# A two-block model on one core: first weights moved ahead of x, their second half behind it

## The chip, the cores and the metric

The kernel runs on one core of one Trainium2 chip. The metric is the device time of one execution in microseconds (us). Engines are named as in the profile: PE is TensorE (matmuls; PEld its weight loads), DVE is VectorE, ACT is ScalarE, POOL is GpSimd, SP is SyncE, which issues nearly all DMAs; SPq is its queue. Line numbers are those of the kernel before.

## The reference

One sequence of 512 tokens, 1024 wide, passes two blocks. Only the start of the first concerns this change:

```python
def rmsnorm(x, g):
    y = xf * rsqrt(mean(xf * xf, -1) + 1e-6)
    return y * g
...
h = rmsnorm(x, norm1_g)
u = h @ w_in
...
```

`w_in` is 1024 by several thousand; its columns feed a short convolution, three kinds of attention or state mixing, and gates. After that come an output product, a gated FFN of width 2816, and a second block with windowed attention and spatial gating. All is float32.

## The kernel before

**Products.** x is kept turned: features on the 128 partitions, tokens along the row, as eight blocks of 128x512. Each float32 product is made of three in a rounded type: with w = whi + wlo and h = hh + hl, a tile is the sum over eight blocks of whi·hh + whi·hl + wlo·hh, so 24 matmuls of 128x512 accumulate in one PSUM bank. ACT makes whi (a rounding copy of raw), POOL makes wlo = raw - whi.

**Units.** Weights come in units of 1024 rows by 256 columns (1 MB) into `raw`, which has two slots. A unit has two column halves of 128 columns, each one tile. Unit n uses slot n % 2; SP loads it when `lo_done` says that POOL is through with the slot's last content (`slot_free`). ACT rounds unit n in `split(n)` (line 1142), POOL makes its rest in `rest` (line 528), one count of `lo_done` for each column half. PE works tile after tile (`gemm_fm`, lines 596, 597 and 604), after `hi_done` and `lo_done`. The row scale of the norm is not put on h: PE multiplies x times g, and the scale (rcol, as R in every lane) is multiplied on each tile afterwards.

**The beginning**, which the change touches. x arrives in four pieces (`load_x(q)`, line 357, 512 KB each, semaphore `x_in{q}`), each with the columns of two blocks. PE turns block m of x (`turn_in(m)`, line 673, four transposes) into the bank TURN[m]: the banks are M[0] to M[3], G[1], G[2], G[3] and M[0] again, so block 7 can be turned only when block 0 has been copied out of M[0]. ACT makes hh of the block (line 1172), DVE makes hl (line 1574); these read the bank. Besides, each turned block is copied to xT, unscaled, for later: blocks 0, 4, 5 and 6 by DVE (line 1577, `xg_kept`), the others by ACT (line 1177, `x_kept`).

Unit 0 is special. The first column half of its weights comes in two parts of four row blocks each (`first_weights(q)`, line 370, 256 KB, `first_raw{q}`), which ACT rounds separately (line 1170, `first_hi`), POOL following (line 546). The second column half (line 361, 512 KB, `raw_in0`) is rounded in one piece (line 1174, `hi_done`). SP issues in the order of its program; it holds x's third piece until the first has landed, the fourth until the second has, and the second column half until `first_raw1`; unit 1's 1 MB follows right behind that.

PE's beginning is written out in `first_tile`: nine idle products on a zeroed tile (line 681), blocks 0 and 1, two idle products, blocks 2 and 3, two idle products, then the products of the first tile (lines 703, 704) in the order of k, with blocks 4 and 5 turned ahead of k = 2, and 6 and 7 ahead of k = 4. The parts of whi are waited for at k = 0 and k = 4. From k = 6 on the products with wlo come in between (line 701), after `lo_done`. Then `gemm_fm(1, ...)` computes the second column half, whose first product is the first of line 596; its bank G[1] held turned block 4.

Of the kernel before, what the change touches and what calls it, by code (L numbers as in the profile page):

```python
# [29 lines left out]
KD = DM // P  # L30
# [45 lines left out]
def build_program(nc, x, par, cst1, cst2a, w_in, w_branch, w_o, w_gu, w_down, w_in2, sg_w, sg_b, ln_g,  # L76
                  ln_b, w_ao, w_so, w_o2, out):
    f32, f32r = mybir.dt.float32, mybir.dt.float32r
    ALU, ACT = mybir.AluOpType, mybir.ActivationFunctionType
# [5 lines left out]
    with ctx:  # L85
# [269 lines left out]
        def _(sp):  # L355
# [13 lines left out]
            def first_weights(q):  # L369
                sp.dma_start(raw[:, 0, 4 * q:4 * q + 4, 0:P], cols(w_in, IN_XA, P, 4 * q, 4)).then_inc(sem(f"first_raw{q}"), 16)  # L370

            load_x(0)
            load_x(1)
            first_weights(0)
            sp.wait_ge(sem("x_in0"), 16)
            load_x(2)
            first_weights(1)
            sp.wait_ge(sem("x_in1"), 16)
            load_x(3)
            sp.wait_ge(sem("first_raw1"), 16)  # L380
            load(0, cols(w_in, IN_XA + P, P), raw[:, 0, :, P:])
            for n, c in enumerate(a_cols):
# [193 lines left out]
        def _(pe):  # L576
            mm = nc.tensor.matmul

            def gemm_fm(T, n, s, xh, xl, kts, col, first, whi_=whi, wlo_=wlo, hooks=None, ready=None):

                bank = bank_of(T) if isinstance(T, int) else G[T[1]]
                Tv = T if isinstance(T, int) else T[0]
                if not isinstance(T, int) or T >= 4:

                    pe.wait_ge(sem("tile_free"), free_before(T) if isinstance(T, int) else Tv - 3)
                else:
                    pe.wait_ge(sem("xg_kept"), T + 1)
                if first:

                    pe.wait_ge(sem("hi_done"), n + 1)  # L590
                for k in range(kts):
                    if ready:

                        pe.wait_ge(sem(ready[0]), ready[1] + k + 1)
                    w = whi_[:, s, k, col:col + P]
                    mm(bank[:, :], w, xh[:, k, :], start=(k == 0), stop=False)  # L596
                    mm(bank[:, :], w, xl[:, k, :], start=False, stop=False)  # L597
                    if hooks and 2 * k + 2 in hooks:
                        hooks[2 * k + 2]()
                if whi_ is whi:  # L600

                    pe.wait_ge(sem("lo_done"), 2 * n + 1 + col // P)
                for k in range(kts):
                    last = mm(bank[:, :], wlo_[:, s, k, col:col + P], xh[:, k, :], start=False, stop=(k == kts - 1))  # L604
                    if hooks and 2 * kts + k + 1 in hooks:
                        hooks[2 * kts + k + 1]()
                last.then_inc(sem("tile_done"), 1)
# [60 lines left out]
            def turn_in(m):  # L668
                pe.wait_ge(sem(f"x_in{m // 2}"), 16)
                if m == KD - 1:  # L670
                    pe.wait_ge(sem("xg_kept"), 1)
                for t in range(TT):
                    last = nc.tensor.transpose(TURN[m][:, t * P:(t + 1) * P], xtm[:, t, m * P:(m + 1) * P], ident)
                last.then_inc(sem("xT_ps"), 1)

            def first_tile():

                bank = G[0]
                def idle_products(count):
                    for i in range(count):  # L680
                        mm(bank[:, 0:P], warm, warm, start=True, stop=True)

                pe.wait_ge(sem("warm"), 1)
                idle_products(9)
                pe.wait_ge(sem("ident_in"), 16)
                for m in range(2):
                    turn_in(m)
                idle_products(2)
                for m in range(2, 4):
                    turn_in(m)  # L690
                idle_products(2)
                for k in range(KD):
                    if k in (2, 4):
                        turn_in(k + 2)
                        turn_in(k + 3)
                    if k in (0, 4):
                        pe.wait_ge(sem("first_hi"), k // 4 + 1)
                    if k == KD - 2:
                        pe.wait_ge(sem("lo_done"), 1)
                    for i in {KD - 2: range(0, 4), KD - 1: range(4, KD - 1)}.get(k, ()):  # L700
                        mm(bank[:, :], wlo[:, 0, i, 0:P], hh[:, i, :], start=False, stop=False)
                    pe.wait_ge(sem("h_lo"), k + 1)
                    mm(bank[:, :], whi[:, 0, k, 0:P], hh[:, k, :], start=(k == 0), stop=False)
                    mm(bank[:, :], whi[:, 0, k, 0:P], hl[:, k, :], start=False, stop=False)
                mm(bank[:, :], wlo[:, 0, KD - 1, 0:P], hh[:, KD - 1, :], start=False, stop=True).then_inc(sem("tile_done"), 1)
# [154 lines left out]
            for n in range(N_A):  # L860
                def after(j, n=n):
                    if n == 1 and j == 0:

                        pe.wait_ge(sem("c1_in"), 16)
                        pe.wait_ge(sem("x_kept"), KD - 4)
                        pe.wait_ge(sem("rcol"), 1)
                        for t in range(TT):
                            last = nc.tensor.transpose(M[0][:, t * P:(t + 1) * P], rcol[:, t:t + 1].broadcast_to((P, P)), ident)
                        last.then_inc(sem("r_ps"), 1)
                    run_mix(stages, 2 * n + j)  # L870
                if N_VV <= n < N_VV + 2:
                    wide_unit(n, n - N_VV, tiles_before(N_VV), lambda t: after(t // 2) if t % 2 else None)
                elif n == 0:
                    first_tile()
                    gemm_fm(1, 0, 0, hh, hl, KD, P, True)
                else:
                    unit_fm(n, after=after)
# [247 lines left out]
        def _(act):  # L1125
# [38 lines left out]
            act.preload_act_table_set(EXP_LN)  # L1164
            act.wait_ge(sem("start_in"), 16)
            for m in range(KD):
                if m in (2, 4):
                    q = m // 2 - 1
                    act.wait_ge(sem(f"first_raw{q}"), 16)
                    fn(whi[:, 0, 4 * q:4 * q + 4, 0:P], raw[:, 0, 4 * q:4 * q + 4, 0:P], ACT.Copy).then_inc(sem("first_hi"), 1)  # L1170
                act.wait_ge(sem("xT_ps"), m + 1)
                fn(hh[:, m, :], TURN[m][:, :], ACT.Copy, scale=pcol("g1", m)).then_inc(sem("h_hi"), 1)
            act.wait_ge(sem("raw_in0"), 16)
# [362 lines left out]
        def _(dve):  # L1536
# [35 lines left out]
            for m in range(KD):  # L1572
                dve.wait_ge(sem("h_hi"), m + 1)
                stt(out=hl[:, m, :], in0=TURN[m][:, :], scalar=pcol("g1", m), in1=as_f32(hh[:, m, :]),
                    op0=ALU.mult, op1=ALU.subtract).then_inc(sem("h_lo"), 1)
                for g in {1: (0,), KD - 1: (4, 5, 6)}.get(m, ()):
                    v.tensor_copy(xT[:, g, :], TURN[g][:, :]).then_inc(sem("xg_kept"), 1)

            ts(half_c, pcol("cw", 0, 20), 0.5, None, ALU.mult)
# [653 lines left out]
```

## Time and profile before

| | us |
|---|---|
| median of three runs | 1326.94 (1326.91 to 1326.95) |
| the profiled execution, its own time | 1327.24 |
| its span, first to last instruction | 1325.2 |
| PE busy | 1317.9 |
| POOL busy | 594.0 |
| DVE busy | 575.6 |
| ACT busy | 510.4 |

The profile was taken in one execution. Its span is from the first to the last instruction; the execution's own time is 2.0 us longer. Engines work side by side, so busy times do not add up to the span. PE is busy 99% of it, so the time of this kernel is PE's row of products and the gaps in it.

### The profile page before, as it was taken

The numbers are of one execution on the slowest core, as the hardware profiler recorded it, in microseconds if no ns is written. First come the engines' busy times: TensorE is split into PE (matmuls) and PEld (weight loads), VectorE is DVE, ScalarE is ACT, GpSimd is POOL, SyncE is SP. The second block draws the span as 40 slices with busy tenths as digits, with TensorE's granted clock in tenths as the row PEclk, the third lists the DMA queues.
The fourth block names the chain that finished last, engine by engine and source line by source line (L and its number), as shares of the span: only waits on it lengthen the run. The fifth ranks groups of instructions, "written<-read, shape, count | busy, mean of one in ns | idle before, by whom it ended". The sixth has DMA issues, their size and how long they took to land.

```text
span 1325.2 us, 16981 instructions
## 1 busy us (share of the span) xinstructions
PE 1317.9 (99%) x6504; PEld 1080.5 (82%) x6504; DVE 575.6 (43%) x952; ACT 510.4 (39%) x731; POOL 594.0 (45%) x448
## 2 busy tenths in 40 slices
PE   9999999999999999999999999999999999999998
PEld 8877877888888888888888888877778888888887
DVE  4674544556544333313321345666555322242233
ACT  6223534566433433222211235354555224343233
POOL 4453333443644364444544555433433453435441
PEclk9999999999999999999999999999999999999999
DMA  6333142313223343333333223322222232423321
GB/s 203 96 113 102 43 148 68 124 41 119 80 94 137 95 113 103 100 97 96 95 96 95 87 72 112 104 69 75 94 68 90 95 95 64 127 65 97 99 90 64
DMA packets 144494, 126.70 MB, mean 96 GB/s; under 512 B 4465, under 2 KB 139761, under 8 KB 144433
## 3 DMA queue, kind: packets, MB, share of 16 engines
q1 hardware_dynamic: 144080, 125.66, 30.9%
q8 instruction: 43, 0.70, 0.2%
q10 hardware_dynamic: 352, 0.19, 0.1%
q14 instruction: 19, 0.15, 0.0%
HBM read 120.46 MB, written 2.10 MB: 92 GB/s over the span
## 4 chain that ended last, share of the span: by engine, by line
PE 99%; DMA 1%; ACT 0%; ACTq 0%; SPq 0%; DVE 0%; issue 0%
PE gemm L596 26%; PE gemm L597 26%; PE gemm L604 26%; PE gemm L657 2%; PE gemm L654 2%; PE gemm L653 2%; PE gemm L620 2%; PE gemm L621 2%; PE gemm L626 2%; PE mix L990 1%; PE mix L978 1%; PE mix L967 1%; DMA xtm<-x 1%; PE mix L1044 1%; PE mix L812 1%; PE mix L837 0%
## 5 line engine op out<-in xcount | busy, mean ns | idle before, releaser
L528 POOL TENSOR_TENSOR wlo<-raw,whi 128x512 fp32r<-128x512 f32 x424 | 568.8, 1372 | 549.3 <-ACT whi L1142 549.3
L596 PE MATMUL gemm<-hh,whi 128*128 128x512 f32 x1128 | 443.9, 394 | 0.0
L597 PE MATMUL gemm<-hl,whi 128*128 128x512 f32 x1128 | 439.4, 390 | 0.0
L604 PE MATMUL gemm<-hh,wlo 128*128 128x512 f32 x1128 | 280.2, 390 | 0.0
L1142 ACT ACTIVATE whi<-raw 128x2048 fp32r<-128x2048 f32 x106 | 202.7, 1912 | 201.3 <-PE gemm L604 167.5
L596 PEld LDWEIGHTS gemm<-hh,whi 128*128 128x128 f32 x1128 | 211.8, 188 | 47.9 <-issue 4.2
L597 PEld LDWEIGHTS gemm<-hl,whi 128*128 128x128 f32 x1128 | 211.9, 188 | 43.1 <-issue 0.2
L604 PEld LDWEIGHTS gemm<-hh,wlo 128*128 128x128 f32 x1128 | 211.3, 188 | 43.6
L524 POOL TENSOR_TENSOR wlo_b<-raw_b,whi_b 128x512 fp32r<-128x512 f32 x16 | 20.6, 1288 | 144.8 <-ACT whi L1142 144.8
L1875 DVE TENSOR_TENSOR fu_t<-gemm,R 128x512 f32<-128x512 f32 x22 | 15.2, 692 | 99.7 <-PE gemm L604 99.7
L596 PE MATMUL gemm<-ah,whi 128*128 128x512 f32 x132 | 51.3, 389 | 0.0
L597 PE MATMUL gemm<-al,whi 128*128 128x512 f32 x132 | 51.3, 389 | 0.0
L1818 DVE TENSOR_TENSOR gt<-gemm,R 128x512 f32<-128x512 f32 x32 | 22.1, 690 | 65.2 <-PE gemm L604 65.0
L1159 ACT ACTIVATE gt<-gt 128x512 f32<-128x512 f32 x32 | 20.1, 628 | 71.6 <-DVE gt L1818 71.6
L1340 ACT ACTIVATE fg_t<-fg_t 128x512 f32<-128x512 f32 x22 | 13.9, 633 | 84.7 <-DVE fg_t L1873 84.7
L1894 DVE TENSOR_TENSOR xT<-xT,gemm 128x512 f32 x16 | 10.9, 688 | 70.1 <-PE gemm L604 56.7
L620 PE MATMUL gemm<-whi,hh 128*128 128x512 f32 x96 | 39.1, 408 | 0.0
L621 PE MATMUL gemm<-whi,hl 128*128 128x512 f32 x96 | 37.6, 391 | 0.0
L1882 DVE TENSOR_TENSOR al<-fu_t,ah 128x512 f32 x22 | 34.7, 1575 | 2.7
L1873 DVE TENSOR_TENSOR fg_t<-gemm,R 128x512 f32<-128x512 f32 x22 | 15.2, 692 | 46.4 <-PE gemm L604 39.8
L604 PE MATMUL gemm<-ah,wlo 128*128 128x512 f32 x132 | 32.9, 389 | 0.0
L1385 ACT ACTIVATE wp<-mix,sml 128x256 f32<-128x256 f32 (+1 forms) x64 | 27.8, 455 | 10.5 <-DVE sml L1973 10.5
(454 smaller groups left out, 1854.9 us busy)
## 6 DMA issues: line engine op xcount, KB each, us to landing
raw<-w_in SPq DMA_DIRECT2D x53, 1024.0 KB, 5.3
raw<-w_gu SPq DMA_DIRECT2D x44, 512.0 KB, 5.0
raw<-w_o SPq DMA_DIRECT2D x8, 1024.0 KB, 5.1
raw<-w_down SPq DMA_DIRECT2D x16, 512.0 KB, 3.9
raw_b<-w_branch SPq DMA_DIRECT2D x16, 256.0 KB, 5.8
raw<-w_ao SPq DMA_DIRECT2D x4, 1024.0 KB, 5.1
raw<-w_so SPq DMA_DIRECT2D x4, 1024.0 KB, 5.1
raw<-w_in SPq DMA_DIRECT2D x7, 512.0 KB, 4.6
```

The lines of the kernel that those rows point to most:

```text
L528: last = nc.gpsimd.tensor_tensor(a(wlo), a(raw), as_f32(a(whi)), ALU.subtract)
L596: mm(bank[:, :], w, xh[:, k, :], start=(k == 0), stop=False)
L597: mm(bank[:, :], w, xl[:, k, :], start=False, stop=False)
L604: last = mm(bank[:, :], wlo_[:, s, k, col:col + P], xh[:, k, :], start=False, stop=(k == kts - 1))
L620: mm(o, hh[:, 4 * half + i, tok], w, start=(half == 0 and i == 0), stop=False)
L621: mm(o, hl[:, 4 * half + i, tok], w, start=False, stop=False)
L626: last = mm(o, hh[:, 4 * half + i, tok], w, start=False, stop=(half == 1 and i == 3))
L653: mm(bank[:, :], w, xh[:, k, :], start=(k == 0), stop=False)
L654: mm(bank[:, :], w, xl[:, k, :], start=False, stop=False)
L1142: fn(a(whi), a(raw), ACT.Copy).then_inc(sem("hi_done"), 1)
L1385: last = fn(wp[:, s % 3, h, w_from(s):], w_score[:, h, e, w_from(s):], ACT.Exp, bias=w_min(v)[:, h, e:e + 1], accum_out=w_sums(v)[:, h, e, ...
L1882: tt(flat(al), fu_t[:, s, :], as_f32(flat(ah)), ALU.subtract).then_inc(sem("act_lo"), 1)
```

## The change

SP's order of issue at the start; the places at which ACT rounds the two parts of the first weights; who copies turned block 0 (ACT instead of DVE), with the semaphore that says so; and two idle products less. The counts that others wait for are adapted.

```diff
+            first_weights(0)
             load_x(0)
             load_x(1)
-            first_weights(0)
             sp.wait_ge(sem("x_in0"), 16)
             load_x(2)
-            first_weights(1)
             sp.wait_ge(sem("x_in1"), 16)
             load_x(3)
+            first_weights(1)
             sp.wait_ge(sem("first_raw1"), 16)
             load(0, cols(w_in, IN_XA + P, P), raw[:, 0, :, P:])
...
-                    pe.wait_ge(sem("xg_kept"), T + 1)
+                    pe.wait_ge(sem("xg_kept"), T)
...
                 if m == KD - 1:
-                    pe.wait_ge(sem("xg_kept"), 1)
+                    pe.wait_ge(sem("x_kept"), 1)
...
                 for m in range(2, 4):
                     turn_in(m)
-                idle_products(2)
                 for k in range(KD):
...
-                        pe.wait_ge(sem("x_kept"), KD - 4)
+                        pe.wait_ge(sem("x_kept"), KD - 3)
...
             for m in range(KD):
-                if m in (2, 4):
-                    q = m // 2 - 1
+                if m in (0, 6):
+                    q = m // 6
                     act.wait_ge(sem(f"first_raw{q}"), 16)
                     fn(whi[:, 0, 4 * q:4 * q + 4, 0:P], raw[:, 0, 4 * q:4 * q + 4, 0:P], ACT.Copy).then_inc(sem("first_hi"), 1)
+                if m == 4:
+                    act.wait_ge(sem("h_lo"), 1)
+                    fn(xT[:, 0, :], TURN[0][:, :], ACT.Copy).then_inc(sem("x_kept"), 1)
...
-                for g in {1: (0,), KD - 1: (4, 5, 6)}.get(m, ()):
+                for g in (4, 5, 6) if m == KD - 1 else ():
                     v.tensor_copy(xT[:, g, :], TURN[g][:, :]).then_inc(sem("xg_kept"), 1)
```

What SP issues from its first DMA on (line 370 is a part of the first weights, line 357 a piece of x, line 361 the second column half and then unit 1; names in brackets are the semaphores waited for). Before:

```order
L357 DMA xtm<-x 128x4x256 x2
L370 DMA raw<-w_in 128x4x128
L357 DMA xtm<-x 128x4x256 [waits x_in0]
L370 DMA raw<-w_in 128x4x128
L357 DMA xtm<-x 128x4x256 [waits x_in1]
L361 DMA raw<-w_in 128x8x128 [waits first_raw1]
L361 DMA raw<-w_in 128x8x256
```

And in the changed kernel:

```order
L370 DMA raw<-w_in 128x4x128
L357 DMA xtm<-x 128x4x256 x2
L357 DMA xtm<-x 128x4x256 [waits x_in0]
L357 DMA xtm<-x 128x4x256 [waits x_in1]
L370 DMA raw<-w_in 128x4x128
L361 DMA raw<-w_in 128x8x128 [waits first_raw1]
L361 DMA raw<-w_in 128x8x256
```

The first part of the weights is now ahead of all of x, the second behind all of it; the two line-361 transfers still follow the second part.

What ACT does from its first weight or block on, up to the rounding of the second column half (line 1170 rounds a part of the first weights, 1172 a turned block, 1174 the second column half, 1177 copies to xT). Before:

```order
L1172 ACTIVATE hh<-mix,prm 128x512 [waits xT_ps,start_in]
L1172 ACTIVATE hh<-mix,prm 128x512 [waits xT_ps]
L1170 ACTIVATE whi<-raw 128x4x128 [waits first_raw0]
L1172 ACTIVATE hh<-mix,prm 128x512 [waits xT_ps] x2
L1170 ACTIVATE whi<-raw 128x4x128 [waits first_raw1]
L1172 ACTIVATE hh<-gemm,prm 128x512 [waits xT_ps] x3
L1172 ACTIVATE hh<-mix,prm 128x512 [waits xT_ps]
L1174 ACTIVATE whi<-raw 128x8x128 [waits raw_in0]
```

And in the changed kernel, where the same lines are 1169 (parts of the first weights), 1174 (blocks), 1172 (the copy to xT that is new here) and 1176 (second column half):

```order
L1169 ACTIVATE whi<-raw 128x4x128 [waits first_raw0,start_in]
L1174 ACTIVATE hh<-mix,prm 128x512 [waits xT_ps] x4
L1172 ACTIVATE xT<-mix 128x512 [waits h_lo]
L1174 ACTIVATE hh<-gemm,prm 128x512 [waits xT_ps] x2
L1169 ACTIVATE whi<-raw 128x4x128 [waits first_raw1]
L1174 ACTIVATE hh<-gemm,prm 128x512 [waits xT_ps]
L1174 ACTIVATE hh<-mix,prm 128x512 [waits xT_ps]
L1176 ACTIVATE whi<-raw 128x8x128 [waits raw_in0]
```

The rounding of the first part moved from behind block 1 to ahead of block 0, that of the second from behind block 3 to behind block 5, and the copy of block 0 stands ahead of block 4.

## Rows read from the trace of the kernel before

**Rows 1.** The page: span, PE's busy time, the chain by engine.

```profile
span 1325.2 us, 16981 instructions
...
PE 1317.9 (99%) x6504; PEld 1080.5 (82%) x6504; DVE 575.6 (43%) x952; ACT 510.4 (39%) x731; POOL 594.0 (45%) x448
...
PE 99%; DMA 1%; ACT 0%; ACTq 0%; SPq 0%; DVE 0%; issue 0%
```

**Rows 2.** The chain in order of time, 0 to 60 us: start, us, what.

```profile
1.27 5.48 DMA xtm<-x
6.76 4.89 DMA xtm<-x
11.70 0.66 PE gemm L673 x4
```

**Rows 3.** PE and PEld timelines: start, us, engine, line, operation [idle before <-releaser].

```profile
5.18 1.81 PE L673 MATMUL mix<-c,xtm 128*128 128x128 f32 x8
...
7.28 1.04 PE L673 MATMUL mix<-c,xtm 128*128 128x128 f32 x8
8.15 0.61 PE L681 MATMUL gemm<-warm 128*128 128x128 f32 x4
...
11.69 0.42 PEld L673 LDWEIGHTS gemm<-c,xtm 128*128 128x128 f32 x4 [0.63 <-DMA xtm<-x]
...
11.70 0.66 PE L673 MATMUL gemm<-c,xtm 128*128 128x128 f32 x4 [0.20 <-DMA xtm<-x]
...
13.56 1.08 PE L701 MATMUL gemm<-hh,wlo 128*128 128x512 f32 x4
...
16.30 0.39 PE L596 MATMUL gemm<-hh,whi 128*128 128x512 f32 x1
```

**Rows 4.** SP timeline: when each DMA was issued.

```profile
5.06 0.37 SPq L357 DMA_DIRECT2D xtm<-x  x1
...
6.76 0.37 SPq L357 DMA_DIRECT2D xtm<-x  x1
9.92 0.99 SPq L361 DMA_DIRECT2D raw<-w_in  x2
...
18.53 6.68 SPq L361 DMA_DIRECT2D raw<-w_in  x2
```

**Rows 5.** DMA answers, issues at 0.7, 5.0, 6.7, 9.9, 10.3, 18.5 us: xcount, KB, us to landing.

```profile
c<-cst ACTq DMA_DIRECT2D x1, 64.0 KB, 2.7
...
xtm<-x SPq DMA_DIRECT2D x1, 512.0 KB, 4.1
...
xtm<-x SPq DMA_DIRECT2D x1, 512.0 KB, 4.9
...
raw<-w_in SPq DMA_DIRECT2D x1, 512.0 KB, 4.9
...
raw<-w_in SPq DMA_DIRECT2D x1, 1024.0 KB, 7.4
...
raw<-w_in SPq DMA_DIRECT2D x1, 1024.0 KB, 5.3
```

**Rows 6.** ACT timeline, 9 to 17 us.

```profile
9.93 0.63 ACT L1170 ACTIVATE whi<-raw 128x512 fp32r<-128x512 f32 x1 [0.53 <-DMA raw<-w_in]
...
14.80 1.06 ACT L1174 ACTIVATE whi<-raw 128x1024 fp32r<-128x1024 f32 x1 [1.15 <-DMA raw<-w_in]
15.77 2.04 ACT L1177 ACTIVATE xT<-mix 128x512 f32<-128x512 f32 x4
```

**Rows 7.** Stretches: PE, PEld, DVE, ACT, POOL busy (xcount), PEclk, DMA share, GB/s.

```profile
11.00:12.00 1.00, 0.80 (x6) 0.37 (x5) 0.83 (x2) 0.72 (x2) 0.92 (x1) 1.00 0.63 139
...
12.00:16.30 4.30, 4.30 (x25) 3.63 (x23) 3.77 (x7) 2.77 (x5) 0.35 (x1) 1.00 1.09 349
```

**Rows 8.** POOL timeline: the rest of the first weights' second part.

```profile
10.64 1.29 POOL L546 TENSOR_TENSOR wlo<-raw,whi 128x512 fp32r<-128x512 f32 x1 [1.03 <-ACT whi L1170]
```

**Rows 9.** DVE timeline: hl of block 7.

```profile
13.78 0.74 DVE L1574 SCALAR_TENSOR_TENSOR hl<-mix,prm,hh 128x512 fp32r<-128x512 f32 x1
```

## The prediction

> **What bounds the kernel now.** The page comes first: its busy shares and its chain of waits. TensorE is busy 99% of the 1325.2 us span, and the chain that ended last is 99% TensorE and 1% DMA [rows 1]. So almost all of the time is a fixed row of matmuls, and an edit of the beginning can only change how soon that row runs without a gap. The chain in order of time says where the gaps are: it starts with the first two pieces of x landing at 6.75 us, goes on through the last piece of x (issued at 6.76, landed at 11.65), and from 11.70 on is TensorE alone [rows 2]. The timeline by engine gives the rest: TensorE turns x, multiplies the first column half of unit 0 (G[0]), and starts the second column half (G[1], line 596) at 16.30 with no gap in front [rows 3]. What matters is therefore one number: when line 596 first starts. After it the work of TensorE is the same before and after. In the trace of before it needs two things by 16.30: the end of the first tile, and the second half of unit 0's columns, transferred and rounded. That transfer was issued at 9.92, when the first weights' second part had landed [rows 4], took 4.9 us [rows 5], and ScalarE rounded it from 14.80 to 15.86 [rows 6]. It was ready 0.44 us ahead of its use. That is the slack that I look at most.
>
> **How long transfers take.** Everything in question is issued by SyncE and moves in the order of issue. With work in the queue the rate is 349 GB/s (12.0 to 16.3 us) [rows 7], so 256 KB (262 kB) cost 0.75 us and 512 KB 1.5 us of a full queue. A transfer issued into an idle queue pays more: the 1 MB issued at 18.53 took 5.3 us [rows 5], of which 3.0 are its bytes at that rate and 2.3 are not.
>
> **The change part by part.**
> *Weights ahead of x.* 256 KB move ahead of x's first two pieces. By bytes these land 0.75 us later; since the queue is still filling up then, it may be 1.0. I take 0.85: the first piece, whose landing let SyncE go on at 5.06, lands at 5.9, the second, which did so at 6.76 [rows 4], at 7.6. The rounding of these weights (as long as that of their second part, 0.63 us) [rows 6] now lies in front of x's first turned block, in time in which ScalarE is idle: nothing.
> *x's third and fourth piece* are issued on those landings, so at 5.9 and 7.6. Before, the third took 4.1 us with 256 KB of weights still in front of it [rows 5]; now the queue runs out before it, since a new issue takes some 2.3 us to flow. From an idle queue 512 KB cost 5.3 - 1.5 = 3.8 us. So it lands at 9.7 to 10.0. The fourth took 4.9 us with 256 KB of weights between [rows 5]; without them 4.15 from 7.6 is 11.75, and one full-queue piece behind the third gives 11.2. I take 11.45 against 11.65: what is won by taking 256 KB out from in front of it is nearly all lost by issuing it 0.85 later. This is the step at which I expect the hoped-for gain to vanish.
> *The second part of the first weights* is now issued behind it. It lands one 256 KB step later, 12.2; before it landed at 9.9 (ScalarE began at 9.93) [rows 6]. Three engines feel this. ScalarE, 0.63 us: 12.85, with the last two turned blocks (6 and 7) queued behind that wait. GpSimd, 1.29 us [rows 8]: 14.15. TensorE can start its correction products (line 701) only then; before it started them at 13.56 and needed 2.74 us from there to line 596 [rows 3]. So the first tile ends at 14.2 + 2.75 = 16.95, 0.65 later than before. The rest of the feed keeps up: block 6 is rounded at 13.5, block 7 at 14.2, VectorE's halves take 0.74 each [rows 9], so block 7 is whole at about 15.0, and TensorE wants it at 16.0.
> *The second column half of unit 0* is issued on that landing: 12.2 instead of 9.92, 2.28 us later. It is the same transfer (same 512-byte pieces, with the same 1 MB right behind it), so I take the same 4.86 us: landed 17.05, rounded (1.06) 18.1. Bounds from rows: at most the 5.3 that a transfer of twice its size took, at least 5.3 - 1.5 = 3.8 by bytes. Line 596 starts at about 18.1 instead of 16.30: 2.28 less the 0.44 of slack is 1.84 us. **It takes the place of the end of the first tile**, so the 0.65 isn't added to it.
> *The Trainium skill speaks for less.* The page "DMA: Bandwidth & Descriptors", section "Anatomy of one DMA — SWDGE (gpsimd) path", gives a DMA as about 2.0 us plus bytes at 436 GB/s, for the other issuing path. By that 512 KB are an estimated 3.2 us, line 596 would wait for the tile's end alone, and the sum would be +0.65. The trace disagrees for this transfer (4.9 us), and the sum goes by the trace.
> *First turned block copied by ScalarE.* 0.5 us (2.04 for four) [rows 6] between blocks 3 and 4, at about 9.8, where ScalarE waits for x's third piece anyway; VectorE loses a copy of the same size, which stood between blocks 1 and 2 in its queue and comes off nothing that TensorE waits for. The bank of block 0 is then free long before block 7 needs it at 12. Nothing.
> *Two idle products less* (begun at 8.15) [rows 3]: the products behind them now wait for block 0's halves until 8.5 or so anyway. Nothing.
> *Behind line 596.* What is late next is unit 1: its 1 MB took 7.4 us [rows 5] and landed at about 17.75, so it now lands at 20.0, ScalarE rounds it until 22.0, TensorE (shifted by 1.8) wants it at 23.6. The sums of squares and the scale end at about 27.2, wanted at 29.0. GpSimd's parts have over 1 us each. SyncE's next load (18.53 before) [rows 4] goes out about 2.3 later and lands at 26; ScalarE, itself about 2 us later with the rest of the opening, comes to it after 28. From there ScalarE waits for TensorE again. All hidden.
>
> **Sum.** +1.8 us. The profiled execution took 1327.24 us (span 1325.2), so 1329.0 for such a one; it lies 0.3 above the median of the three runs, 1326.94, so the forecast for the median is 1328.8. This is +0.14%. What a measurement of this kernel can tell from no change I put at 0.2%, 2.65 us, so all of this is likely "within".
>
> **The rivals.**
> *Second half hidden by the first tile.* If the transfer issued at 12.2 takes 3.8 us (its bytes off the 5.3 row), it lands at 16.0 and is rounded at 17.1; the end of the first tile at 16.95 decides nearly alone: +0.65 to +0.95, about 1327.8. For: nothing else is in flight then. Against: before, hardly anything was in flight either (0.63 of the 16 engines' time from 11 to 12 us) [rows 7] and it took 4.9.
> *x sooner, the other side.* x's last piece is the last DMA on the chain, and TensorE's weight loads sat idle 0.63 us before its blocks [rows 3]. If taking 256 KB out from in front of it brings it 0.8 us forward (10.85), the tile could end at 15.5, and the time is 1326.1, faster. The point from which it decides: the second column half must be rounded by then, so it must land 14.4, 2.4 us after an issue at about 12. No row is under 2.7 us, and that one is 64 KB [rows 5]. Hardly possible in full; in part it is the low end of my range.
> *The clock.* The first eight turning products took 1.81 us together, the next eight 1.04 [rows 3]: TensorE was at half pace at first, though the granted clock of the windows says 1.00 throughout [rows 7]. The stall of about 1.1 us that I expect before line 596 might bring half pace back; 16 products of 0.227 us would then cost 3.6 us more, 1332.4. Against: the short waits around 11.6, 0.20 us of products and 0.63 of weight loads [rows 3], left the pace of the products behind them as it was. It decides only if the clock falls within that stall.
> *The change does nothing*: the transfers shift but each is covered. It would need the second column half to land by 15.3. No row lets it.
>
> **How the numbers follow.** Forecast 0.68 (own range: the late transfer from 4.4 to 5.3 us and the landing of the weights from 11.9 to 12.7, so +1.1 to +2.8: 1328.0 to 1329.8). Hidden by the tile 0.17. x sooner or no effect 0.07. Clock 0.08. The range reaches from the bottom of the second case and a little of the third to the top of the first: 1327.2 to 1329.9. Slower by over 0.2% (above 1329.6): the clock and the uppermost part of the forecast, 0.13. Faster by over 0.2% (under 1324.3): more than every wait of TensorE up to 16 us gives back together, 0.01. Within: 0.86.
>
> **What would show it.** In the profile of the changed kernel: x's last piece landed between 11.2 and 11.7; ScalarE's second rounding of first weights at about 12.2 after a wait for DMA; ScalarE's 128x1024 rounding (14.80 before) at about 17 after a wait for DMA; TensorE idle about 1.1 us before its first line-596 product, with that rounding as releaser; the same product at 18.1; from there everything shifted by one constant. I am wrong if that product waits for nothing, or starts before 17.3, or if the shift grows after it.

## The result and the profile after

| | before | changed |
|---|---|---|
| median, 22 runs each | 1326.94 | 1328.95 |
| lowest and highest | 1326.83, 1327.48 | 1328.52, 1329.91 |
| the profiled execution | 1327.24 | 1328.55 |
| its span | 1325.2 | 1326.5 |

The ratio is 1.0015, 95% interval 1.0009 to 1.0021: 2.0 us slower, within the 0.2% that the prediction called no change, and within its range. The runs of the changed kernel spread over 1.4 us, those of before over 0.65. The profiled execution is among the fastest of the changed kernel, and that of before lies 0.3 above its own median, so the two traces show 1.31 us of the 2.0.

The page of the changed kernel, with the same rows as [rows 1]:

```profile
span 1326.5 us, 16973 instructions
...
PE 1318.7 (99%) x6500; PEld 1081.3 (82%) x6500; DVE 574.6 (43%) x951; ACT 511.0 (39%) x732; POOL 593.9 (45%) x448
...
PE 99%; DMA 0%; ACT 0%; POOL 0%; ACTq 0%; issue 0%; SPq 0%; DVE 0%
```

At this level only the chain has changed, and hardly: POOL has entered it, and the 1% of DMA is now 0%. The chain in order of time, which answers to [rows 2], shows more (start, us, what):

```profile
1.26 4.50 DMA xtm<-x
...
5.90 1.94 PE mix L673 x8
...
11.53 1.27 ACT hh L1174 x2
12.80 0.52 ACT whi L1169
13.39 1.30 POOL wlo L546
14.74 1.20 PE gemm L700 x4
```

Before, the chain went from x's last piece straight to PE. Now it goes from x's first piece through PE's turning products to ACT, which rounds blocks 4 and 5 (line 1174) and only then the weights' second part (1169); POOL makes the rest of that part, and PE starts the first four correction products (line 700, which was 701) at 14.74. The PE timeline, against [rows 3]:

```profile
5.90 1.94 PE L673 MATMUL mix<-c,xtm 128*128 128x128 f32 x8 [0.63 <-DMA xtm<-x]
...
8.49 1.64 PE L673 MATMUL mix<-c,xtm 128*128 128x128 f32 x8
...
14.74 1.20 PE L700 MATMUL gemm<-hh,wlo 128*128 128x512 f32 x4
...
17.61 0.40 PE L596 MATMUL gemm<-hh,whi 128*128 128x512 f32 x1
```

Line 596 starts at 17.61 instead of 16.30, without a gap in front of it. The difference, 1.31 us, is also the difference of the two profiled executions (1328.55 - 1327.24): behind this point nothing moved in these two executions. In all of the profiles that follow, the execution's time less the start of line 596 is between 1310.92 and 1311.06, close to before's (1327.24 - 16.30 = 1310.94), but for two that are named.

The ACT timeline, against [rows 6]:

```profile
12.69 0.63 ACT L1169 ACTIVATE whi<-raw 128x512 fp32r<-128x512 f32 x1
...
16.31 1.06 ACT L1176 ACTIVATE whi<-raw 128x1024 fp32r<-128x1024 f32 x1 [1.72 <-DMA raw<-w_in]
```

The second column half was rounded at 17.37, 0.24 before its use. SP's issues, against [rows 4], and the time to landing of that half (DMA answer for issues at 12.4), against [rows 5]:

```profile
1.26 6.27 SPq L357 DMA_DIRECT2D xtm<-x  x4
7.58 0.51 SPq L370 DMA_DIRECT2D raw<-w_in  x1
12.38 0.99 SPq L361 DMA_DIRECT2D raw<-w_in  x2
```

```profile
raw<-w_in SPq DMA_DIRECT2D x1, 512.0 KB, 3.9
```

It was issued 2.46 us later than before, and took 3.9 us instead of 4.9. The rate while the queue ran out of work (columns as in [rows 7]):

```profile
6.00:8.00 2.00, 2.00 (x10) 2.00 (x11) 0.14 (x1) 0.81 (x2) 0.28 (x1) 1.00 0.68 214
```

That is 214 GB/s, where a queue that always had work moved 349 [rows 7].

### The profile page after: what moved, and what is told of

Read it like the earlier page. It is cut to its first block, busy times and chain, and to the rows that moved or that the text cites. A ratio compares the mean times of both kernels' runs of the same rounds, so it can differ in the third digit from the quotient of the medians.

```text
span 1326.5 us, 16973 instructions
## 1 busy us (share of the span) xinstructions
PE 1318.7 (99%) x6500; PEld 1081.3 (82%) x6500; DVE 574.6 (43%) x951; ACT 511.0 (39%) x732; POOL 593.9 (45%) x448
## 4 chain that ended last, share of the span: by engine, by line
PE 99%; DMA 0%; ACT 0%; POOL 0%; ACTq 0%; issue 0%; SPq 0%; DVE 0%
PE gemm L596 26%; PE gemm L597 26%; PE gemm L604 26%; PE gemm L657 2%; PE gemm L654 2%; PE gemm L653 2%; PE gemm L620 2%; PE gemm L621 2%; PE gemm L626 2%; PE mix L989 1%; PE mix L977 1%; PE mix L966 1%; PE mix L1043 1%; PE mix L811 1%; PE mix L836 0%; PE mix L794 0%
```

## The experiments

Three things of this trace had to be told apart. **W**: the second part of the first weights comes late, and everything from it to the end of the first tile hangs on it. **S**, the prediction's: the second column half decides. **P**: TensorE keeps half pace until about 9.7 us (16 turning products take 1.94 and 1.64 us, before 1.81 and 1.04 [rows 3]), by this theory because it idles before x's first piece. The kernels ran in three groups, each on one chip beside the kernel before, the second and third on the same chip. The medians are told against that of before in the same group, since it moved between groups (1327.22, 1327.33 and 1326.97). A difference of under 0.5 us between kernels of different groups is not read.

### First group: the change again, its two halves, and the pace

`a0_change_again` is the changed kernel, for a second trace.

> The changed kernel once more, for a second profile: its runs spread over 1.4 us (1328.5 to 1329.9) where those of before spread over 0.6. Theory P (pace): the spread is the moment at which TensorE's products go from half to full pace; the idle gap before x's first piece leaves that to chance, so this profile may show the change of pace at another moment than 9.7 us, and the start of line 596 moves with it (17.3 to 18.6). Theory W (weights): the start of line 596 hangs on the landing of the first weights' second part alone, so it stays at 17.6 +- 0.3 and the spread comes from the DMAs. Time by both 1328.5 to 1329.9.

Measured: 1328.68 (1328.18 to 1329.15) against 1327.22, ratio 1.0009 (1.0000 to 1.0019), so +1.5 us. Its PE timeline:

```profile
6.53 1.06 PE L673 MATMUL mix<-c,xtm 128*128 128x128 f32 x8 [1.26 <-DMA xtm<-x]
...
7.88 1.04 PE L673 MATMUL mix<-c,xtm 128*128 128x128 f32 x8
...
13.28 0.50 PE L702 MATMUL gemm<-hh,whi 128*128 128x512 f32 x1 [0.29 <-ACT whi L1169]
...
14.65 1.19 PE L700 MATMUL gemm<-hh,wlo 128*128 128x512 f32 x4 [0.18 <-POOL wlo L546]
...
17.60 0.47 PE L596 MATMUL gemm<-hh,whi 128*128 128x512 f32 x1
```

Here the pace is full from the first turning product on, x's first piece came 0.6 later, and line 596 starts at the same time, 17.60. The waits stand at the weights' second part (ACT's rounding, then POOL's rest). That speaks for W, against P as the cause of this delay. It speaks against the reason given in P too: TensorE idled 1.26 us before x's first piece here and had full pace, 0.63 us in the trace above and had half.

`a1_second_behind_x` is before with this alone:

```diff
             load_x(2)
-            first_weights(1)
             sp.wait_ge(sem("x_in1"), 16)
             load_x(3)
+            first_weights(1)
...
-                if m in (2, 4):
-                    q = m // 2 - 1
+                if m in (2, 6):
+                    q = m // 6
```

> Before, with only the second part of the first weights put behind x's last piece (and rounded behind block 5). x's first pieces land as before, so the pace changes at about 6.7 us and the first product of line 703 starts near 8.5. Theory W: the second part lands at about 12.1, rounded 12.8, its rest 14.1, line 596 at 17.0 to 17.3: 1326.94 + 0.7 to 1.0 = 1327.6 to 1327.9. Theory P: line 596 at 16.3 to 16.5, 1326.9 to 1327.1. Should x's last piece land at 11.0 instead of 11.65, the part lands at 11.7 and W gives +0.4.

Measured: 1328.34, ratio 1.0008 (0.9999 to 1.0018), +1.1 us. ACT, POOL and PE:

```profile
12.19 0.63 ACT L1170 ACTIVATE whi<-raw 128x512 fp32r<-128x512 f32 x1 [0.38 <-DMA raw<-w_in]
...
17.24 0.47 PE L596 MATMUL gemm<-hh,whi 128*128 128x512 f32 x1
```

As W said, and a little more (+1.1 for 0.7 to 1.0), since the part was rounded from 12.19. From the start of the rounding to line 596 are 5.05 us; in `a0_change_again`, where the rounding started at 12.59, 5.01. So a nearly fixed time follows on the landing of the weights' second part.

`a2_first_ahead_of_x` is before with the other move alone:

```diff
+            first_weights(0)
             load_x(0)
             load_x(1)
-            first_weights(0)
...
-                if m in (2, 4):
-                    q = m // 2 - 1
+                if m in (0, 4):
+                    q = m // 4
```

> Before, with only the first part of the first weights put ahead of x (and rounded ahead of block 0). Theory P: TensorE idles 0.6 us before x's first piece, keeps half pace beyond block 1, and the first product of line 703 starts at 9.6 to 9.9 instead of 8.52; from there 24 products and 16 turnings need 7.2 us, so line 596 starts at 17.0 or later: 1327.7 to 1328.3, with a spread of over 0.8 us between runs. Theory W: the second part of the weights is in time, line 596 at 16.3 to 16.7: 1326.9 to 1327.3.

Measured: 1328.21 (1327.66 to 1328.73), ratio 1.0007 (0.9997 to 1.0016), +1.0. Its trace, of an execution of 1327.76:

```profile
8.62 0.48 PE L703 MATMUL gemm<-hh,whi 128*128 128x512 f32 x1
...
12.24 0.66 PE L673 MATMUL gemm<-c,xtm 128*128 128x128 f32 x4 [0.59 <-DMA xtm<-x]
...
16.84 0.39 PE L596 MATMUL gemm<-hh,whi 128*128 128x512 f32 x1
```

The median is what P said, but the trace gives another reason: the first product stands at 8.62 in full pace, and what is late is x's last piece, on which PE waits until 12.24 (11.70 before). Line 596 is late by the same 0.54. W, which gave 1327.3 at most, missed this. With 256 KB ahead of x, SP issued x's last piece at 7.30 instead of 6.76, and it landed as much later. The ten runs fall in two groups, five from 1327.66 to 1327.99 and five from 1328.44 to 1328.73. None of the upper five was profiled, so what delays those is not shown, and P is not excluded for them.

`a3_more_idle` is the changed kernel with `idle_products(11)` instead of 9.

> The changed kernel with 11 idle products at the very start instead of 9, which fill the gap up to x's first piece (5.27 to 5.90). Theory P: full pace from about 6.7 us in every run, blocks 2 and 3 turned in 1.0 us instead of 1.6, the first product of the first tile at about 9.2 instead of 9.9; line 596 then waits for the weights' second part at about 17.3; the median falls by 0.3 to 0.8 to 1328.1 to 1328.6 and the spread shrinks to under 0.8. Theory W: nothing but noise, 1328.8 to 1329.1 with the same spread.

Measured: 1328.44 (1328.09 to 1328.79), ratio 1.0008 (0.9998 to 1.0017): 0.24 under `a0_change_again` in the same group, its spread 0.70 against 0.97. Inconclusive for P: the difference is in its sense and under its lower end, and both profiles had the full pace early.

```profile
5.96 1.06 PE L673 MATMUL mix<-c,xtm 128*128 128x128 f32 x8 [0.30 <-DMA xtm<-x]
...
17.08 0.47 PE L596 MATMUL gemm<-hh,whi 128*128 128x512 f32 x1
```

In this trace the weights' second part landed early, and was rounded from 12.06; line 596 follows 5.02 us later.

These 5.0 us do not yet tell W from S. SP issues the second column half when the weights' second part lands, so both chains start at the same moment, and in three of these four traces they end within 0.15 us of each other. In `a0_change_again` the half was rounded at 17.45, and TensorE loaded its weights for line 596 right behind that:

```profile
16.39 1.06 ACT L1176 ACTIVATE whi<-raw 128x1024 fp32r<-128x1024 f32 x1 [2.01 <-DMA raw<-w_in]
```

```profile
17.57 0.19 PEld L596 LDWEIGHTS gemm<-hh,whi 128*128 128x128 f32 x1 [0.31 <-issue]
```

The product starts 0.03 us after that load; in the trace of before, where nothing held the load, it started 0.22 after it:

```profile
16.08 0.19 PEld L596 LDWEIGHTS gemm<-hh,whi 128*128 128x128 f32 x1
```

In `a0_change_again`, `a1_second_behind_x`, `a3_more_idle` and `b2_change_ungated` (below) line 596 starts 0.14 or 0.15 us behind the end of that rounding, the same distance as in the two runs below whose profile names the rounding as the releaser, and its first product takes 0.47 us instead of 0.39. So in these four the half came last, by about 0.1 us, although the profile names no wait. The second group moves the two chains apart.

### Second group: the second column half, the queue, and the small edits

`b1_half_on_x_in3` is the changed kernel with

```diff
             first_weights(1)
-            sp.wait_ge(sem("first_raw1"), 16)
+            sp.wait_ge(sem("x_in3"), 16)
             load(0, cols(w_in, IN_XA + P, P), raw[:, 0, :, P:])
```

> The changed kernel, but the second column half is issued when x's last piece has landed, about 0.7 us sooner than on the first weights' second part. Theory S (what the prediction said: the second column half decides): line 596 starts earlier by what that transfer gains, up to 0.6 us, so the median falls by 0.3 to 0.6 under the changed kernel's 1328.7. Theory W (the first weights' second part decides: its landing plus 5.05 us is the start of line 596, through its rounding, GpSimd's rest and the correction products): the half is rounded at 16.8 instead of 17.4, TensorE doesn't notice or gains under 0.15: 1328.5 to 1328.8.

Measured: 1328.29 (1327.89 to 1329.01) against 1327.33, ratio 1.0009 (1.0000 to 1.0018), +1.0.

```profile
12.38 0.63 ACT L1169 ACTIVATE whi<-raw 128x512 fp32r<-128x512 f32 x1 [0.24 <-DMA raw<-w_in]
...
15.53 1.06 ACT L1176 ACTIVATE whi<-raw 128x1024 fp32r<-128x1024 f32 x1 [1.36 <-DMA raw<-w_in]
...
17.29 0.39 PE L596 MATMUL gemm<-hh,whi 128*128 128x512 f32 x1
```

The half is rounded at 16.59, and line 596 still starts at 17.29, 0.7 later, directly behind the tile; the rounding of the weights' second part lies 4.91 before it, 0.1 less than in the runs above. So in the changed kernel as it is, the half costs 0.1 or so on its own: the start of line 596 speaks for W. The median lies where S had put it (1328.1 to 1328.4), but that forecast counted from the first group's 1328.7, and 0.4 can't be read across groups.

`b2_change_ungated` is the changed kernel without the two waits between x's pieces:

```diff
             load_x(1)
-            sp.wait_ge(sem("x_in0"), 16)
             load_x(2)
-            sp.wait_ge(sem("x_in1"), 16)
             load_x(3)
```

> The changed kernel without SyncE's waits for x's first two pieces, so that x's third and fourth piece and the weights' second part are in the queue before it runs dry. Theory W with the queue as the cause: the rate no longer dips between 6 and 8 us, x's last piece lands at about 10.9 instead of 11.6, the second part at 11.6 instead of 12.4, line 596 at 16.6 to 16.9, the median about 0.8 under the changed kernel: 1327.7 to 1328.1. If the queue's gap costs nothing (the transfers share the same rate anyway): 1328.5 to 1328.9.

Measured: 1327.74 (1327.16 to 1329.39), ratio 1.0005 (0.9996 to 1.0014), +0.4. The rate from 6 to 8 us and the start of line 596 (594 here):

```profile
6.00:8.00 2.00, 1.66 (x16) 1.47 (x14) 0.80 (x2) 1.27 (x2) 0.19 (x1) 1.00 1.09 372
```

```profile
16.20 0.47 PE L594 MATMUL gemm<-hh,whi 128*128 128x512 f32 x1
...
823.50 0.47 PE L594 MATMUL gemm<-hh,whi 128*128 128x512 f32 x1
```

372 GB/s instead of 214: the queue's gap was the cost. Line 596 starts 0.1 earlier than before's 16.30 (0.4 earlier than W had said), so in this execution all of the change's loss, and in the median most of it, hangs on the late issue of x's third and fourth piece. Two of the eleven runs took 1329.02 and 1329.39; neither was profiled. This is one of the two executions that lost something later: at 823.5, the start of the second block, PE waits 0.23 us for unit weights that ACT had rounded only at 823.36.

```profile
821.44 1.92 ACT L1139 ACTIVATE whi<-raw 128x2048 fp32r<-128x2048 f32 x1 [5.53 <-DMA raw<-w_in]
```

`b3_before_ungated` is before without the same two waits.

> Before, without SyncE's waits for x's first two pieces; order of issue unchanged. x's last piece, which ends the wait of TensorE at 11.65, lands at 11.1 or earlier if the dips of the rate at 9 and 11 us come from late issue; line 596 then starts at 15.9 instead of 16.3 and the median falls by 0.2 to 0.5 under before's 1327.2. If the first piece loses by sharing the queue, or if the second column half (0.44 us of slack) holds line 596, no gain: within 0.15 of before.

Measured: 1327.30 (1327.04 to 1327.43), ratio 1.0000 (0.9991 to 1.0009), no difference. x's last piece landed 0.2 sooner, and line 596 started at 16.10:

```profile
11.53 0.62 PE L671 MATMUL gemm<-c,xtm 128*128 128x128 f32 x4
...
16.10 0.39 PE L594 MATMUL gemm<-hh,whi 128*128 128x512 f32 x1
```

In before the weights between x's pieces keep the queue at work: it moved 321 GB/s from 6 to 8 us, with the waits, where the changed kernel moved 214.

```profile
6.00:8.00 2.00, 2.00 (x17) 2.00 (x16) 0.79 (x2) 1.63 (x3) 0.00 (x0) 1.00 1.09 321
```

So its waits cost nearly nothing. The same waits cost about 1 us in the changed order.

`b4_copy_and_idle_only` is before with the copy of block 0 by ACT and without the two idle products: the change without its transfers.

```diff
-                idle_products(2)
...
+                if m == 4:
+                    act.wait_ge(sem("h_lo"), 1)
+                    fn(xT[:, 0, :], TURN[0][:, :], ACT.Copy).then_inc(sem("x_kept"), 1)
...
-                for g in {1: (0,), KD - 1: (4, 5, 6)}.get(m, ()):
+                for g in (4, 5, 6) if m == KD - 1 else ():
```

The counts of `xg_kept` and `x_kept` that others wait for are those of the changed kernel.

> Before, with only what the change does besides the weights: ScalarE copies turned block 0 (between blocks 3 and 4) and the two idle products ahead of the first tile's products are gone. By the prediction both cost and give nothing: within 0.15 us of before. If the idle products kept TensorE's pace up, or if the copy delays block 4: up to 0.6 slower. If DVE's freed 0.7 us brings the halves of blocks 2 and 3 forward on the path: up to 0.3 faster.

Measured: 1327.73 (1327.54 to 1328.62), ratio 1.0004 (0.9995 to 1.0013), +0.4: not nothing.

```profile
10.05 0.63 ACT L1169 ACTIVATE whi<-raw 128x512 fp32r<-128x512 f32 x1 [0.63 <-DMA raw<-w_in]
10.58 0.58 ACT L1172 ACTIVATE xT<-mix 128x512 f32<-128x512 f32 x1
11.06 1.84 ACT L1174 ACTIVATE hh<-gemm,prm 128x512 fp32r<-128x512 f32 x3
```

```profile
11.78 2.07 DVE L1576 SCALAR_TENSOR_TENSOR hl<-gemm,prm,hh 128x512 fp32r<-128x512 f32 x3 [1.50 <-ACT hh L1174]
```

In before's order the copy stands right behind the rounding of the weights' second part, and blocks 4, 5 and 6 follow without a pause. DVE gets block 4 at 11.78, in before at 11.17 (0.12 of this is the later landing of that part), and so PE's products of block 4 start at 12.67, in before at 12.54, although x's last piece landed 0.2 earlier. Line 596 started at 16.54, +0.24. The missing idle products are not in this: the first tile's first product started at 8.31, 0.2 sooner than before, at full pace. Behind line 596 this execution lost 0.25 more, most of it at 823 us, as the one of `b2_change_ungated`. In the changed order the copy stands at 10.76, ahead of blocks that PE turned only from 10.89 on, and delays nothing.

### Third group: two limits together, and a version without them

`c0_split_rest` is the changed kernel with the first four correction products on a semaphore of their own and ahead of block 4's products:

```diff
                     last = nc.gpsimd.tensor_tensor(a(wlo), a(raw), as_f32(a(whi)), ALU.subtract)
+                    if j == 0 and k == 0:
+                        last.then_inc(sem("lo_first"), 1)
...
+                    if k == 4:
+                        pe.wait_ge(sem("lo_first"), 1)
+                        for i in range(4):
+                            mm(bank[:, :], wlo[:, 0, i, 0:P], hh[:, i, :], start=False, stop=False)
                     if k in (0, 4):
                         pe.wait_ge(sem("first_hi"), k // 4 + 1)
-                    if k == KD - 2:
+                    if k == KD - 1:
                         pe.wait_ge(sem("lo_done"), 1)
-                    for i in {KD - 2: range(0, 4), KD - 1: range(4, KD - 1)}.get(k, ()):
-                        mm(bank[:, :], wlo[:, 0, i, 0:P], hh[:, i, :], start=False, stop=False)
+                        for i in range(4, KD - 1):
+                            mm(bank[:, :], wlo[:, 0, i, 0:P], hh[:, i, :], start=False, stop=False)
```

> The changed kernel, but the first four correction products no longer wait for GpSimd's rest of the weights' second part: they wait for the rest of the first part alone and stand ahead of the products of block 4, where TensorE waits for the second part anyway. Theory W: the first tile ends 0.5 to 1.0 us sooner, at 16.2 to 16.7, and then the second column half, rounded at about 17.4, becomes the one that line 596 waits for: start 17.45, TensorE idle before it with ScalarE's rounding as releaser, a gain of only 0.1 to 0.2 over the changed kernel: 1328.3 to 1328.7. If the second column half were no limit, line 596 would start at 16.8: 1327.8.

Measured: 1329.10 (1328.52 to 1329.66) against 1326.97, ratio 1.0016 (1.0007 to 1.0025), +2.1; the profile is of the lowest run, 1328.52.

```profile
16.09 0.39 PE L710 MATMUL gemm<-hh,wlo 128*128 128x512 f32 x1
17.50 0.47 PE L598 MATMUL gemm<-hh,whi 128*128 128x512 f32 x1 [1.02 <-ACT whi L1182]
17.81 0.40 PE L599 MATMUL gemm<-hl,whi 128*128 128x512 f32 x1
```

```profile
16.30 1.06 ACT L1182 ACTIVATE whi<-raw 128x1024 fp32r<-128x1024 f32 x1 [2.16 <-DMA raw<-w_in]
```

The first tile now ends 1.3 us sooner, and nothing is won: PE stands idle 1.02 us for the rounding of the second column half, and line 596 starts at 17.50. That is the picture that the prediction had drawn of the change. The start came within 0.05 us of what was expected. The median lies 0.4 above the expected range; why, the profile of the lowest run can't say.

`c1_split_rest_half_sooner` has in addition the earlier issue of `b1_half_on_x_in3`.

> The same, with the second column half issued on the landing of x's last piece as well. Theory W with both limits taken away: the half is rounded at 16.6, the tile ends at 16.2 to 16.6, line 596 at about 16.65: 1327.5 to 1327.8, 0.6 to 1.0 under the changed kernel. Each of the two edits alone gave under 0.4; together they give what neither gives. If something else holds (pace, x's halves): no more than 0.4.

Measured: 1328.37 (1328.13 to 1328.88), ratio 1.0010 (1.0001 to 1.0019): 0.7 under `c0_split_rest`, in the same group. In its profile x's last piece came at 12.0 and the half still decides:

```profile
17.11 0.47 PE L598 MATMUL gemm<-hh,whi 128*128 128x512 f32 x1 [0.22 <-ACT whi L1182]
```

`b1_half_on_x_in3` had rounded the half sooner with no wait for it; here, with the tile out of the way, the same edit gives 0.7 in the median and 0.4 in the start of line 596. The level of 1327.5 to 1327.8 was missed.

`c2_change_all_queued` is the split with every transfer of the beginning issued without a wait, in the order of the change.

> The split correction products, and SyncE issues everything of the beginning without any wait: first part of the weights, x in four pieces, second part, second column half, unit 1. x's last piece lands at 10.5, the second column half at about 13. Line 596 then hangs on TensorE's own work from the first product on (8.4 + 7.2 us) = 15.6 to 15.9 instead of before's 16.3: 0.4 to 0.7 under before, 1326.6 to 1326.9. If the later loads slow x down in the shared queue, x's last piece lands at 11.5 and the gain is under 0.2.

Measured: 1327.66 (1326.64 to 1328.63), ratio 1.0005 (0.9995 to 1.0014), +0.7 in the median, but its fastest run is 0.14 faster than the fastest of the 33 runs of before (1326.78). That run was profiled:

```profile
11.97 1.17 PE L697 MATMUL gemm<-hh,wlo 128*128 128x512 f32 x4
...
15.70 0.39 PE L595 MATMUL gemm<-hh,whi 128*128 128x512 f32 x1
```

Line 596 (595 here) starts at 15.70 as expected, 0.6 before that of before, bound by PE's own work. The forecast of the median failed: eleven runs spread over 2.0 us.

`c3_before_all_queued` is the same with before's order of transfers.

> Before's order of the transfers, issued without any wait, with the split correction products placed ahead of the turning of blocks 6 and 7, where TensorE waits for x's last piece. x's last piece lands at 11.4 as in the run of before without waits; from there blocks 6 and 7 are turned (0.9) and 12 products follow (2.75) with the halves of block 7 ready at 14.3: line 596 at 15.4 to 15.9, bounded below by TensorE's own 7.2 us from its first product at 8.6: 1326.6 to 1326.9. If the second column half comes too late for that: 1327.1.

Measured: 1327.07 (1327.00 to 1327.31), ratio 1.0001 (0.9992 to 1.0010). No gain:

```profile
11.12 1.08 PE L695 MATMUL gemm<-hh,wlo 128*128 128x512 f32 x4
12.04 0.60 PE L672 MATMUL gemm<-c,xtm 128*128 128x128 f32 x4
...
14.20 0.50 PE L706 MATMUL gemm<-hh,whi 128*128 128x512 f32 x1 [0.20 <-DVE hl L1577]
...
16.16 0.40 PE L595 MATMUL gemm<-hh,whi 128*128 128x512 f32 x1
```

x's last piece was there at 11.5, but the correction products put ahead of the turning ran until 12.04, and the turning waited for them. Block 6 then reaches PE from DVE only at 14.2, and PE has no other work left there. No version that is reliably faster than before was found.

## Why the prediction was right, and where it was not

**The size and its place.** +1.8 us forecast, +2.0 measured in the median. In the profiled execution it is +1.31 (1328.55, where the prediction gave 1329.0 for such a one), and there all of it lies before line 596, as said. But the prediction had named a sign of being wrong, and it came: the product of line 596 waited for nothing in this trace. That the forecast of the median is this close is in part luck, since 0.7 us of the measured 2.0 stand in no trace (see below).

**x's pieces.** The last one landed at about 11.7 (11.45 forecast, 11.65 before) and the weights' second part at about 12.36 (12.2 forecast; SP went on at 12.38): the gain of 256 KB less in front was lost by the later issue. `b2_change_ungated` shows this cause directly. Two sizes of it were off and mostly cancelled: the last piece was issued at 7.2, not 7.6, and took 4.5 us, not 3.85.

**The step that was mis-sized** is "I take the same 4.86 us" for the second column half. It took 3.9, and ScalarE's rounding ended at 17.37, not 18.1. The bound from the other side, 3.8 by bytes, was much the nearer. In twelve of the fourteen profiles this transfer was issued on an earlier landing; ten times it took 3.7 to 3.9 us, and 4.9 and 5.1 in the profiles of before and of `a2_first_ahead_of_x`. So 4.9 belonged to single executions and not to the transfer; why those two were slower is not shown. With before's order of transfers it took 3.9 in `b4_copy_and_idle_only` and 3.7 in `b3_before_ungated`; x's last piece was still in flight at its issue in both, as it was in before (139 GB/s from 11 to 12 us [rows 7], where the prediction had seen hardly anything in flight), so that alone is not the reason. The Trainium skill's fixed cost plus bytes ("DMA: Bandwidth & Descriptors", "Anatomy of one DMA — SWDGE (gpsimd) path"), given for the other issuing path and an estimated 3.2 us here, was below all twelve, if closer to the usual value than the row I used; its sum of +0.65 was still short.

**The end of the first tile** was put at 16.95 and came at 17.61. The landing was 0.16 later than forecast, ACT began the rounding 0.33 after it because blocks 4 and 5 stood in front (they had been turned late: the half pace of that execution), POOL started 0.07 after ACT's end, and from the correction products to line 596 there were 2.87 us, not 2.75. The forecast had the second column half 1.15 us behind the tile's end; in the trace it was 0.24 ahead. Two errors of about 0.7 each way brought in the rival "second half hidden by the first tile", at 1.3 instead of 0.65 to 0.95.

**What the runs make of the mechanism.** Both limits are real and lie within 0.2 us of each other: with the tile shortened (`c0_split_rest`) the second column half holds line 596 at 17.50; with the half sooner (`b1_half_on_x_in3`) the tile holds it at 17.29. In the changed kernel itself the tile came last in one profile and the half, by about 0.1 us, in the other. The prediction named one and priced the other at 0.65.

**The small edits.** The copy by ACT costs nothing in the order of the change, as forecast, and 0.24 us of the first tile in before's order (`b4_copy_and_idle_only`, in which the trace, and no run of its own, tells the copy from the missing idle products). The clock rival did not come as written: in `c0_split_rest` TensorE stood still for 1.02 us before line 596, the stall that the rival asked for, and the products behind it took 0.47 and 0.40 us, as elsewhere. But half pace lasted to 9.7 us in one of the profiles, and that the prediction had not seen as possible at this place.

**What stays open** is the spread. Kernels that put weights ahead of x spread over 0.7 to 2.2 us, those with x first over 0.3 to 0.4 (`b3_before_ungated`, `c3_before_all_queued`), apart from `a1_second_behind_x` and `b4_copy_and_idle_only` (1.5 and 1.1, through one and two high runs); before itself spread over 0.65 to 1.8 in groups of 22 to 33 runs. Late full pace would make such a spread, and one profile shows it; but no run from the upper end of a spread was profiled, and `a3_more_idle`, made to test it, was inconclusive. The idle time before x's first piece does not order the pace: full pace followed on 1.26 us in `a0_change_again`, half pace on 0.63 in the changed kernel's first profile and on no gap at all in `b3_before_ungated` (1.94 us for its first eight turning products). Of the 2.0 us between the medians, the two profiled executions show 1.31. The other 0.7 has no shown cause: 0.4 lies between the changed kernel's profiled run and its median, 0.3 between those of before.

## What to carry to other kernels

A transfer held back until an earlier one lands cost nothing that could be measured while the queue had other work in front of it (`b3_before_ungated`, ratio 1.0000); if a reorder takes that work away, the same wait opens a gap. When a transfer moves, follow all that is chained to its landing: here its rounding, the rest behind that, and a further transfer. And where two chains end within half a microsecond, price both, expect that shortening one gives nothing, and look whether they start at the same event: then a fixed distance from that event to the product does not say which of them holds it.

## What the runs showed of the hardware that was not expected

- TensorE's change from half to full pace came at different times in executions that did the same work up to there: in the changed kernel 16 turning products took 1.94 + 1.64 us in one profile and 1.06 + 1.04 in the other, although TensorE had idled longer before them there (1.26 us against 0.63). The granted clock of the stretches read 1.00 throughout.
- One and the same 512 KB transfer, issued on an earlier landing, took 3.7 to 3.9 us in ten profiles and 4.9 and 5.1 in two.
- Half-way through the program, at 823 us, there is a second place at which a late weight transfer shows: in two of the executions profiled the first product there started 0.15 and 0.23 us late.
